# Index-score products of the last block: two single products per tile of the second input projection, instead of three in a row at a tile's end

## The chip, the cores and the metric

The program runs on one core of a Trainium2 chip. The metric is the device time of one execution in microseconds (us), as the median of a few runs. The kernel before takes 2761.79 us (three runs, 2760.8 to 2763.72).

The core's engines work side by side and meet only at semaphores. PE is TensorE, the matrix engine (PEld is its weight loading), ACT is ScalarE, DVE is VectorE, POOL is GpSimd and SP is the engine that starts most DMAs.

## The reference, cut to what matters

The program is three transformer-like blocks over 512 tokens of width 1024. The first two have one form, the third another. The third begins like this:

```python
h = rms_norm_2(x, g_mix_pre[l])
(lru_x, lru_gate, pool_in, q, k, v, q_idx, k_idx, w_idx,
 gate_logits) = split_columns(h @ w_in[l], IN_SIZES)
ua = causal_depthwise_conv(lru_x, conv_w[l], conv_b[l])
ya = rg_lru(ua, lru_w_a[l], ...) * jax.nn.gelu(lru_gate)
yb = multiscale_pool(pool_in, w_pool[l], pool_scale[l])
yc = dsa_attention(q, k, v, q_idx, k_idx, w_idx)
```

and inside `dsa_attention`, for each block of 128 queries:

```python
admissible = key_chunk[None, :] <= q_chunk[:, None]      # chunks of 64 keys
logits = jnp.einsum('bqhd,bsd->bqhs', qib, k_idx_f) * (IDX_DIM ** -0.5)
score = jnp.einsum('bqh,bqhs->bqs', wb * (IDX_HEADS ** -0.5), jax.nn.relu(logits))
score = jnp.where(admissible[None], score, -jnp.inf)
_, sel = lax.top_k(score, top_k)                         # top_k = 128
```

There are 8 index heads of width 64 and 4 blocks of 128 queries. Query block b has 128 (b + 1) keys that matter. Block 0 has no more than 128 of them, so that all that are admissible are selected whatever their score is.

## The kernel before, in words

Activations lie transposed (features on partitions, the 512 tokens along the free axis). Each float32 operand of a projection is split into a high and a low part, and one block of 128 x 128 weights costs three matrix products of 512 columns: high x high, high x low, low x high (lines 568 to 570, function `mac`). A tile of the projection is one bank of PSUM with 128 output features. It sums 8 weight blocks, so it is 24 products in a row.

The second input projection is stage "z2": 23 tiles, numbered 0 to 22. Tiles 4 to 7 give the index queries `qi`, tile 8 the index keys `ki`, tile 9 the values and index weights, tiles 10 to 13 the input of the pooling, 14 to 17 the gate of the recurrence, 18 to 21 the attention queries and 22 the attention keys. Four banks are used in turn, and a tile waits until the one four before it was taken out (`free_bank`, `tile_free`). A unit of weights (16 blocks, two tiles) is loaded by SP, its high part is written by ACT (`split_unit`, line 1099) and its low part by DVE (line 1599). In each engine's program these splits stand behind the evacuation of the tile that frees the buffer, so the order of work is written out by hand and each engine takes it strictly in a row.

The index scores are made beside z2 as items t, eight (one for each head) per query block. An item is one product on PE with only 64 rows of contraction (line 987), on partitions 0 to 63 for even heads and 64 to 127 for odd heads. It is as wide as the keys of its block, 128 to 512 columns, and goes to one of two banks in turn (`SCORES[t % 2]`). ACT takes it out with a Relu into one of two slots of `sq` (line 1496), and DVE multiplies it with its head's weight and adds it to `score` (lines 2107 and 2110). Item t waits on PE until the Relu of item t - 2 is done. The Relu of item t waits until DVE has added item t - 2. In the kernel before there are 32 items, three at the end of each of tiles 11 to 20 and two at the end of tile 21, on all three engines (`idx_items`).

From tile 18 on, DVE also takes one round of the selection of the top 128 per tile (`take_top8`). Later, after the z2 stage, `hide(0)` overwrites the whole score of query block 0 with constants, and the selection rounds work on blocks 1 to 3 only.

Behind z2 comes the stage "lru" with 12 short tiles of one block (three products) each. ACT loads a table of functions (line 1498), splits the last unit of z2's buffers (line 1099), and takes out lru tiles 0 to 3 as `yb_hi`; DVE follows with `yb_lo` (line 2167) and frees the bank. The lru tile 4 waits for the bank of lru tile 0. After it come the merges ("bm2").

Of the kernel before, what the change touches and what calls it, by code (L numbers as in the profile page):

```python
# [11 lines left out]
ACT = mybir.ActivationFunctionType  # L12
AX_X = mybir.AxisListType.X

P = 128
S = 512
# [231 lines left out]
def block_kernel(nc, stream, xT, pT, memT, vec1, gains, cst, pos, out):  # L248
    with ExitStack() as ctx:
# [16 lines left out]
        sq = sb("sq", 108, [2, S])  # L266
# [204 lines left out]
        idx_done = sem("idx_done")  # L471
# [44 lines left out]
        }  # L516


        IDX_FROM, IDX_ITEMS = 11, 32

        def idx_items(n):
            return range(min(3 * max(n - IDX_FROM, 0), IDX_ITEMS), min(3 * max(n - IDX_FROM + 1, 0), IDX_ITEMS))
        assert idx_items(22).stop == IDX_ITEMS


        NORMS = {
# [30 lines left out]
        def _(pe):  # L557
# [17 lines left out]
                    pe.wait_ge(tile_free, c.at("T", st, n - 3))  # L575
                return bank[t % 4]

            def run(c, st, operand, first=0, last=None, width=S, after=None, together=None):


                tiles = TILES[st]
                u0 = c.base[st]["U"]
                ends = {}
                for n, t in enumerate(tiles):
                    for j, b in enumerate(t):
                        ends[b // BLK] = (n, j)
                seen = -1 if first == 0 else tiles[first - 1][-1] // BLK
                if together is not None:
                    seen, first = tiles[together][0] // BLK, together + 2
                    pe.wait_ge(lo_ready, c.at("U", st, seen + 1))  # L590
                    two = [free_bank(c, st, together + n)[:, 0:width] for n in range(2)]
                    for j in range(KD):
                        for n in range(2):
                            xh, xl, need = operand(together + n, j)
                            if need is not None:
                                pe.wait_ge(need[0], need[1])
                            mm = mac(two[n], (u0 + seen) % 2, tiles[together + n][j] % BLK, P, xh, xl, j == 0, j == KD - 1)
                            if j == KD - 1:
                                mm.then_inc(tile_done, 1)
                for n in range(first, len(tiles) if last is None else last):  # L600
                    t = tiles[n]
                    ps = free_bank(c, st, n)[:, 0:width]
                    for j, b in enumerate(t):
                        u = b // BLK
                        if u > seen:
                            pe.wait_ge(lo_ready, c.at("U", st, u + 1))
                            seen = u
                        xh, xl, need = operand(n, j)
                        if need is not None:
                            pe.wait_ge(need[0], need[1])  # L610
                        mm = mac(ps, (u0 + u) % 2, b % BLK, P, xh, xl, j == 0, j == len(t) - 1)
                        if j == len(t) - 1:
                            mm.then_inc(tile_done, 1)
                        elif ends[u] == (n, j):
                            mm.then_inc(part_done, 1)
                    if after is not None:
                        after(n)

# [355 lines left out]
            def after_z2(n):  # L974
                if n == 10:
                    pe.wait_ge(act_took, c.at("A", "z2", 5))
                    for t in range(ST):
                        mm = nc.tensor.transpose(TURNED[:, t * P:(t + 1) * P], vwT[:, t * P:(t + 1) * P], ident)
                    mm.then_inc(vw_turned, 1)
                for t in idx_items(n):  # L980
                    if t == 0:
                        pe.wait_ge(tile_free, c.at("T", "z2", 9))
                    if t >= 2:
                        pe.wait_ge(idx_relu, t - 1)
                    b, hh = t // 8, t % 8
                    r = slice(64 * (hh % 2), 64 * (hh % 2) + 64)
                    nc.tensor.matmul(SCORES[t % 2][:, 0:(b + 1) * P], qi[r, hh // 2, b * P:(b + 1) * P], ki[r, 0:(b + 1) * P],  # L987
                                     start=True, stop=True).then_inc(idx_done, 1)
            run(c, "z2", lambda n, j: (h_hi[:, j, :], h_lo[:, j, :], (res_split, c.at("R", "norm1", j + 1)) if n == 4 else None),
                together=4, after=after_z2)  # L990

            def lru_operand(n, j):
                if n < 4:
# [43 lines left out]
        for table, stages in ((RR1, STAGES1), (RR2, STAGES2)):  # L1037
            n = 0
# [36 lines left out]
        def _(act):  # L1075
# [398 lines left out]
            link(nc.scalar.activation(lruc[:, 2, 0:4], lruc[:, 1, 0:4], ACT.Ln, bias=1.0))  # L1474
            nc.scalar.activation(lruc[:, 3, 0:4], ap4, ACT.Relu, scale=-1.0).then_inc(softplus_ready, 1)

            def evac_z2(n):
                if n < 8:
                    take_hi(c, "z2", n, n - 4, qi[:, n - 4, :])
                elif n == 9:  # L1480
                    take_hi(c, "z2", n, 4, vwT[:, :])
                elif 14 <= n < 18:
                    if n == 14:
                        for j in range(4):
                            split_hi(c, "z2", j, ua_hi[:, j, :], ua[:, j, :], (res_ready, result_value(c, "z2", j)))
                    take_hi(c, "z2", n, n - 9, lg[:, n - 14, :], ACT.Gelu_apprx_tanh)
                elif n == 19:
                    for j in range(4):
                        r = c.base["z2"]["R"] + 4 + j
                        split_hi(c, "z2", 4 + j, pool_hi[:, j, :], res[:, r % 4, :], (res_ready, result_value(c, "z2", 4 + j)))  # L1490
                for t in idx_items(n):
                    act.wait_ge(idx_done, t + 1)
                    if t >= 2:
                        act.wait_ge(idx_added, t - 1)
                    w = (t // 8 + 1) * P
                    nc.scalar.activation(sq[:, t % 2, 0:w], SCORES[t % 2][:, 0:w], ACT.Relu).then_inc(idx_relu, 1)
            stage_loop(c, "z2", evac_z2, 2)
            act.preload_act_table_set("sigmoid_and_others")
            split_unit(c, "z2", SPLIT_LATER["z2"])
# [79 lines left out]
        def _(dve):  # L1579
# [518 lines left out]

            def add_idx(t):

                b, hh = t // 8, t % 8
                w = (b + 1) * P
                dve.wait_ge(idx_relu, t + 1)
                if t == 0:
                    dve.wait_ge(res_ready, result_value(c, "z2", 3))
                if hh == 0:
                    ins = nc.vector.tensor_scalar(score[:, b, 0:w], sq[:, t % 2, 0:w], wsc[:, b, hh:hh + 1], None, ALU.mult)
                else:
                    dve.wait_ge(idx_added, t)
                    ins = nc.vector.scalar_tensor_tensor(out=score[:, b, 0:w], in0=sq[:, t % 2, 0:w], scalar=wsc[:, b, hh:hh + 1],  # L2110
                                                         in1=score[:, b, 0:w], op0=ALU.mult, op1=ALU.add)
                ins.then_inc(idx_added, 1)
# [16 lines left out]
            A_Z2 = {n: n - 4 for n in range(4, 8)} | {9: 4} | {n: n - 9 for n in range(14, 18)}  # L2129

            def evac_z2(n):
                if n in A_Z2:
                    dve.wait_ge(act_took, c.at("A", "z2", A_Z2[n] + 1))
                    pass_on(c, "z2", n)
                    if 4 <= n < 8:
                        conv(n - 4)
                    elif n >= 14:
                        if n == 14:
                            dve.wait_ge(tile_free, c.at("T", "z2", 14))
                        pool(n - 14)  # L2140
                elif 10 <= n < 14:
                    if n == 10:
                        dve.wait_ge(pad_ready, 1)
                    copy_out(c, "z2", n, 0, pz[:, n - 10, PADW:PADW + S], lambda ps: ps[:, :], wait_act=False)
                    if n == 10:
                        dve.wait_ge(vw_turned, 1)
                        link(nc.vector.tensor_copy(vw[:, :, :], TURNED[:, :].rearrange("p (t d) -> p t d", t=ST)))

                        link(nc.vector.tensor_scalar(wsc[:, :, :], vw[:, :, HD:HD + 8], 8 ** -0.5, None, ALU.mult))
                else:  # L2150
                    dst = {8: ki, 22: kk}.get(n)
                    if dst is None:
                        scale_out(c, "z2", n, qd[:, n - 18, :], -ATT["dsa"]["scale"])
                    else:
                        copy_out(c, "z2", n, 0, dst[:, :], lambda ps: ps[:, :], wait_act=False)
                for t in idx_items(n):
                    add_idx(t)
                if n >= 18:
                    if n == 18:
                        dve.wait_ge(idx_added, 16)  # L2160
                        hide(1)
                    take_top8(rounds[n - 18])
            stage_loop(c, "z2", evac_z2, 2)
# [426 lines left out]
```

## Time and profile before

| what | value |
|---|---|
| median of three runs | 2761.79 us |
| the profiled execution, its own time | 2761.74 us |
| its span in the trace | 2759.9 us |
| PE busy | 2682.9 us (97%) |
| DVE busy | 1399.2 us (51%) |
| ACT busy | 1120.1 us (41%) |
| mean granted clock of TensorE | 0.995 |

The span is the time between the first and last instruction in the trace; 1.8 us of the execution's own time lie around it. PE is busy nearly all the time, so that what lengthens or shortens PE's row of work, or makes it stand still, is what counts. Starts of matrix products are measured, while their ends are modelled. So the time that one product costs in a stream is read from the start of one to the start of the next.

### The profile page before, as it was taken

The page shows a single profiled execution, that of the slowest core. Times are in us where ns is not written, and L with a number is a line of the kernel's source. Part 1 is how long each engine was busy: PE and PEld are TensorE (multiplying, and loading weights), DVE is VectorE, ACT ScalarE, POOL GpSimd, SP SyncE. Part 2 cuts the span into 40 slices and gives each one's busy share as a digit, 9 for nine tenths or more (in the row PEclk, how much of TensorE's full clock was granted, in tenths as well). Part 3 has the DMA queues.
Part 4 walks back from the last instruction along what each step waited for, and adds up shares of the span by engine and source line. Part 5 has one row for each costly group of instructions (what it writes and reads, how often), then busy time and mean ns, then how long its engine had stood idle before and what let it go on. Part 6 is the DMA issues. An engine that isn't in the chain of part 4 may idle for free. (4 is left out here: it accounts for less than half of the span.)

```text
span 2759.9 us, 34815 instructions
## 1 busy us (share of the span) xinstructions
PE 2682.9 (97%) x13528; PEld 2173.7 (79%) x13528; DVE 1399.2 (51%) x2075; ACT 1120.1 (41%) x1760; POOL 406.4 (15%) x316
## 2 busy tenths in 40 slices
PE   8999999999999899999999999999999999999997
PEld 6876778888887787677898888777687688888886
DVE  6656544533324665654453432465588536533423
ACT  6446533423224644654343222453635535523221
POOL 5100002211102310000131110231001012311101
PEclk9999999999999999999999999999999999999999
DMA  4320123132332232112322233222232222122232
GB/s 155 124 90 32 47 78 121 61 106 91 103 109 93 85 114 86 46 46 77 107 77 91 93 105 107 92 76 92 77 108 91 73 96 77 55 98 91 94 107 90
DMA packets 37501, 245.76 MB, mean 89 GB/s; under 512 B 4608, under 2 KB 5632, under 8 KB 8448
## 3 DMA queue, kind: packets, MB, share of 16 engines
q1 hardware_dynamic: 33632, 239.09, 25.4%
q10 hardware_dynamic: 3744, 4.94, 0.5%
q8 instruction: 87, 1.43, 0.2%
q14 instruction: 38, 0.31, 0.0%
HBM read 241.91 MB, written 2.10 MB: 88 GB/s over the span
## 5 line engine op out<-in xcount | busy, mean ns | idle before, releaser
L568 PE MATMUL bank<-h_hi,w_hi 128*128 128x512 f32 x1928 | 762.2, 395 | 4.7 <-DVEq L1637 3.4
L570 PE MATMUL bank<-h_hi,w_lo 128*128 128x512 f32 x1928 | 751.7, 390 | 0.0
L569 PE MATMUL bank<-h_lo,w_hi 128*128 128x512 f32 x1928 | 751.3, 390 | 0.0
L1599 DVE TENSOR_TENSOR w_lo<-raw,w_hi 128x2048 fp32r<-128x2048 f32 x130 | 300.9, 2317 | 340.1 <-ACT w_hi L1099 339.7
L568 PEld LDWEIGHTS bank<-h_hi,w_hi 128*128 128x128 f32 x1928 | 362.4, 188 | 90.8 <-issue 17.6
L570 PEld LDWEIGHTS bank<-h_hi,w_lo 128*128 128x128 f32 x1928 | 362.2, 188 | 76.3
L569 PEld LDWEIGHTS bank<-h_lo,w_hi 128*128 128x128 f32 x1928 | 362.7, 188 | 73.4 <-issue 1.4
L1099 ACT ACTIVATE w_hi<-raw 128x2048 fp32r<-128x2048 f32 x151 | 287.8, 1910 | 245.6 <-PE bank L570 237.1
L1611 DVE TENSOR_TENSOR w_lo<-raw,w_hi 128x2048 fp32r<-128x2048 f32 x60 | 137.6, 2293 | 156.1 <-ACT w_hi L1328 156.1
L568 PE MATMUL bank<-a_hi,w_hi 128*128 128x512 f32 x528 | 205.4, 389 | 0.0
L569 PE MATMUL bank<-a_lo,w_hi 128*128 128x512 f32 x528 | 205.4, 389 | 0.0
L570 PE MATMUL bank<-a_hi,w_lo 128*128 128x512 f32 x528 | 205.4, 389 | 0.0
L2264 POOL TENSOR_TENSOR a_lo<-res,a_hi 128x512 f32 x66 | 91.3, 1385 | 614.1 <-ACT a_hi L1324 563.9
L1894 DVE TENSOR_TENSOR res<-bank,rstd 128x512 f32<-128x512 f32 x60 | 41.5, 692 | 235.2 <-PE bank L570 235.2
L1324 ACT ACTIVATE a_hi<-res 128x512 f32 x60 | 37.9, 632 | 293.6 <-DVE res L1897 293.6
L2242 POOL TENSOR_TENSOR m_lo<-res,m_hi 128x512 fp32r<-128x512 f32 x24 | 31.0, 1293 | 815.1 <-ACT m_hi L1147 815.1
L1269 ACT ACTIVATE pT<-bank 128x512 f32<-128x512 f32 (+3 forms) x168 | 83.0, 494 | 136.8 <-PE bank L749 133.8
L570 PEld LDWEIGHTS bank<-a_hi,w_lo 128*128 128x128 f32 x528 | 99.1, 188 | 20.7
L568 PEld LDWEIGHTS bank<-a_hi,w_hi 128*128 128x128 f32 x528 | 99.1, 188 | 20.6
L569 PEld LDWEIGHTS bank<-a_lo,w_hi 128*128 128x128 f32 x528 | 99.1, 188 | 20.3
L1328 ACT ACTIVATE w_hi<-raw 128x2048 fp32r<-128x2048 f32 x60 | 114.1, 1901 | 0.0
L1322 ACT ACTIVATE sg<-sg 128x512 f32<-128x512 f32 x60 | 37.9, 632 | 177.1 <-DVE sg L1891 177.1
(430 smaller groups left out, 4575.7 us busy)
## 6 DMA issues: line engine op xcount, KB each, us to landing
raw<-in_stream SPq DMA_DIRECT2D x226, 1024.0 KB, 4.8
x<-in_xT SPq DMA_DIRECT2D x4, 512.0 KB, 8.7
out_T<-x ACTq DMA_DIRECT2D x8, 256.0 KB, 2.1
p_f<-in_pT ACTq DMA_DIRECT2D x2, 512.0 KB, 4.0
memf<-in_memT ACTq DMA_DIRECT2D x1, 1024.0 KB, 5.1
cst_sb<-in_cst ACTq DMA_DIRECT2D x1, 409.0 KB, 7.4
pos_i<-in_pos ACTq DMA_DIRECT2D x1, 258.0 KB, 6.2
g_in<-in_gains ACTq DMA_DIRECT2D x3, 4.0 KB, 2.4
```

The source lines that it names most:

```text
L568: nc.tensor.matmul(ps, wh, xh, start=start, stop=False)
L569: nc.tensor.matmul(ps, wh, xl, start=False, stop=False)
L570: return nc.tensor.matmul(ps, wl, xh, start=False, stop=stop)
L1099: nc.scalar.activation(home(c, v)[0][:, :], raw[v % 2][:, :], ACT.Copy).then_inc(hi_ready, 1)
L1269: nc.scalar.activation(a["pT"][h % 2][:, 0:n, b * P:(b + 1) * P], TURNED[:, 0:n * P].rearrange("p (t q) -> p t q", t=n), ACT.Copy).then_in ...
L1322: nc.scalar.activation(sg[:, p, :], sg[:, p, :], ACT.Silu).then_inc(act_took, 1)
L1324: nc.scalar.activation(a_hi[:, bass.ds(i * 2 + p, 1), :].rearrange("p a s -> p (a s)"), res[:, p, :], ACT.Copy).then_inc(res_hi, 1)
L1328: nc.scalar.activation(w_hi[v][:, :], raw[v][:, :], ACT.Copy).then_inc(hi_ready, 1)
L1599: nc.vector.tensor_tensor(lo[:, :], raw[v % 2][:, :], hi[:, :].bitcast(F32), ALU.subtract).then_inc(lo_ready, 1)
L1611: nc.vector.tensor_tensor(w_lo[s][:, :], raw[s][:, :], w_hi[s][:, :].bitcast(F32), ALU.subtract).then_inc(lo_ready, 1)
L1894: nc.vector.tensor_tensor(res[:, p, :], bank[(t0 + 2 * p + 1) % 4][:, :], rstd[:, 0, :], ALU.mult).then_inc(tile_free, 1)
L2264: nc.gpsimd.tensor_tensor(a_lo[:, bass.ds(i * 2 + p, 1), :].rearrange("p a s -> p (a s)"), res[:, p, :], a_hi[:, bass.ds(i * 2 + p, 1), :] ...
```

## The change

The items of query block 0 are left out (24 items are left, with 256, 384 and 512 columns, eight of each), and `idx_at` gives block and head of an item. Each of the tiles 11 to 22 has two items: one behind weight block j = 3, which is the middle of the tile, and one behind j = 7, its end. PE gets the first through a new hook `within` in `run`. ACT and DVE have the first item ahead of their evacuation of the same tile, and the second behind it.

```diff
-        IDX_FROM, IDX_ITEMS = 11, 32
-        def idx_items(n):
-            return range(min(3 * max(n - IDX_FROM, 0), IDX_ITEMS), min(3 * max(n - IDX_FROM + 1, 0), IDX_ITEMS))
+        IDX_FROM, IDX_ITEMS, IDX_AFTER = 11, 24, (3, 7)
+        def idx_item(n, half):
+            t = 2 * (n - IDX_FROM) + half
+            return [t] if 0 <= t < IDX_ITEMS else []
+        def idx_at(t):
+            return t // 8 + 1, t % 8
...
                             mm.then_inc(part_done, 1)
+                        if within is not None:
+                            within(n, j)
...
-                for t in idx_items(n):
+            def within_z2(n, j):
+                for t in idx_item(n, IDX_AFTER.index(j)) if j in IDX_AFTER else ():
                     if t == 0:
                         pe.wait_ge(tile_free, c.at("T", "z2", 9))
                     if t >= 2:
                         pe.wait_ge(idx_relu, t - 1)
-                    b, hh = t // 8, t % 8
+                    b, hh = idx_at(t)
...
+            def relu_idx(t):
+                act.wait_ge(idx_done, t + 1)
+                if t >= 2:
+                    act.wait_ge(idx_added, t - 1)
+                w = (idx_at(t)[0] + 1) * P
+                nc.scalar.activation(sq[:, t % 2, 0:w], SCORES[t % 2][:, 0:w], ACT.Relu).then_inc(idx_relu, 1)
+
             def evac_z2(n):
+                for t in idx_item(n, 0):
+                    relu_idx(t)
...
-                for t in idx_items(n):
+                for t in idx_item(n, 1):
+                    relu_idx(t)
             stage_loop(c, "z2", evac_z2, 2)
             act.preload_act_table_set("sigmoid_and_others")
...
             def evac_z2(n):
+                for t in idx_item(n, 0):
+                    add_idx(t)
...
-                for t in idx_items(n):
+                for t in idx_item(n, 1):
                     add_idx(t)
                 if n >= 18:
                     if n == 18:
-                        dve.wait_ge(idx_added, 16)
+                        dve.wait_ge(idx_added, 8)
```

The order on PE around the end of tile 11, before (h_hi, h_lo are the activations, w_hi, w_lo the weights of z2, `ki` and `qi` the index keys and queries):

```order
L570 MATMUL bank3<-h_hi_56,w_lo1_54 128x512
L987 MATMUL bank4<-ki_138,qi_136 128x128 [waits tile_free]
L987 MATMUL bank5<-ki_138,qi_136 128x128
L987 MATMUL bank4<-ki_138,qi_136 128x128 [waits idx_relu]
L568 MATMUL bank0<-h_hi_56,w_hi0_51 128x512 [waits lo_ready,tile_free]
```

The three items stand in a row between the last product of one tile and the first of the next. The order on PE now, at the end of one of the later tiles and in the middle of the next:

```order
L996 MATMUL bank5<-ki_138,qi_136 128x512 [waits idx_relu]
L573 MATMUL bank1<-h_hi_56,w_hi0_51 128x512 [waits tile_free]
...
L575 MATMUL bank1<-h_hi_56,w_lo0_53 128x512
L996 MATMUL bank4<-ki_138,qi_136 128x512 [waits idx_relu]
L573 MATMUL bank1<-h_hi_56,w_hi0_51 128x512
L574 MATMUL bank1<-h_lo_57,w_hi0_51 128x512
```

Each item now has full-height products on both sides, and no item has another one next to it.

The order on PE now, at the border of z2's last tile and lru's first (`pool_hi`, `pool_lo` are the operands of lru):

```order
L575 MATMUL bank2<-h_hi_56,w_lo1_54 128x512
L996 MATMUL bank5<-ki_138,qi_136 128x512 [waits idx_relu]
L573 MATMUL bank3<-pool_hi_144,w_hi0_51 128x512 [waits res_split,lo_ready,tile_free]
L574 MATMUL bank3<-pool_lo_145,w_hi0_51 128x512
L575 MATMUL bank3<-pool_hi_144,w_lo0_53 128x512
```

The last item has come to stand behind z2's last tile, where lru's first product followed at once before.

The order on ACT at this border before, from the last items (of tile 21) to the first output of lru:

```order
L1496 ACTIVATE sq_61<-bank4 128x512 [waits idx_added,idx_done]
L1496 ACTIVATE sq_61<-bank5 128x512 [waits idx_added,idx_done]
L1099 ACTIVATE w_hi0_51<-raw0_49 128x2048 [waits raw_ready0,tile_done]
L1498 ACT_TABLE_LOAD
L1099 ACTIVATE w_hi1_52<-raw1_50 128x2048 [waits raw_ready1,tile_done]
L1108 ACTIVATE yb_hi_152<-bank3,cst_sb_70 128x512 [waits tile_done]
```

The order on ACT at the same border now:

```order
L1492 ACTIVATE sq_61<-bank5 128x512 [waits idx_added,idx_done]
L1108 ACTIVATE w_hi0_51<-raw0_49 128x2048 [waits raw_ready0,tile_done]
L1492 ACTIVATE sq_61<-bank4 128x512 [waits idx_added,idx_done]
L1492 ACTIVATE sq_61<-bank5 128x512 [waits idx_added,idx_done]
L1513 ACT_TABLE_LOAD
L1108 ACTIVATE w_hi1_52<-raw1_50 128x2048 [waits raw_ready1,tile_done]
L1117 ACTIVATE yb_hi_152<-bank3,cst_sb_70 128x512 [waits tile_done]
```

Two Relus, those of tile 22's items, have moved between the split of tile 21 and the table load.

## Rows read from the trace of the kernel before

**Rows 1.** Stretches (from:to, length, PE busy, its instructions, granted clock, DMA share, GB/s):
```profile
1886.00:1970.00 84.00, 79.23 (x332) 1.00 0.21 73
```

**Rows 2.** Waits of PE in that stretch (us in total, times, longest):
```profile
PE bank L987 <- ACT sq L1496: 4.8, 10, 0.7
```

**Rows 3.** Timeline of PE, end of tile 11 (start, us, what, idle before):
```profile
1889.99 0.39 PE L570 MATMUL bank<-h_hi,w_lo 128*128 128x512 f32 x1
1890.31 0.49 PE L987 MATMUL bank<-ki,qi 64*128 64x128 f32 x4
1891.16 0.48 PE L987 MATMUL bank<-ki,qi 64*128 64x128 f32 x2 [0.36 <-ACT sq L1496]
1891.58 0.50 PE L568 MATMUL bank<-h_hi,w_hi 128*128 128x512 f32 x1
```

**Rows 4.** Timeline of PE, an item with 256 and one with 384 columns:
```profile
1912.53 0.70 PE L987 MATMUL bank<-ki,qi 64*128 64x256 f32 x2 [0.47 <-ACT sq L1496]
1913.15 0.50 PE L568 MATMUL bank<-h_hi,w_hi 128*128 128x512 f32 x1
...
1935.44 0.91 PE L987 MATMUL bank<-ki,qi 64*128 64x384 f32 x2 [0.57 <-ACT sq L1496]
1936.28 0.50 PE L568 MATMUL bank<-h_hi,w_hi 128*128 128x512 f32 x1
```

**Rows 5.** Timeline of PE, end of tile 19; the first row is of 1949.94 to 1950.00 alone:
```profile
1949.94 0.70 PE L987 MATMUL bank<-ki,qi 64*128 64x512 f32 x2
...
1951.74 1.12 PE L987 MATMUL bank<-ki,qi 64*128 64x512 f32 x2 [0.68 <-ACT sq L1496]
1952.80 0.50 PE L568 MATMUL bank<-h_hi,w_hi 128*128 128x512 f32 x1
```

**Rows 6.** Timeline of PE, end of tile 21 to the first tiles of bm2:
```profile
1966.67 0.39 PE L570 MATMUL bank<-h_hi,w_lo 128*128 128x512 f32 x1
1966.99 1.13 PE L987 MATMUL bank<-ki,qi 64*128 64x512 f32 x4
1968.05 0.50 PE L568 MATMUL bank<-h_hi,w_hi 128*128 128x512 f32 x1
...
1973.41 0.39 PE L570 MATMUL bank<-h_hi,w_lo 128*128 128x512 f32 x1
1973.68 0.47 PE L568 MATMUL bank<-pool_hi,w_hi 128*128 128x512 f32 x1
...
1976.29 0.39 PE L570 MATMUL bank<-pool_hi,w_lo 128*128 128x512 f32 x1
1977.59 0.50 PE L568 MATMUL bank<-ua_hi,w_hi 128*128 128x512 f32 x1 [0.91 <-DVE yb_lo L2167]
...
1983.18 0.39 PE L568 MATMUL bank<-h_hi,w_hi 128*128 128x512 f32 x1
...
1988.62 0.39 PE L568 MATMUL bank<-yb_hi,w_hi 128*128 128x512 f32 x1
```

**Rows 7.** Timeline of ACT, 1968 to 1977 us:
```profile
1968.15 1.09 ACT L1496 ACTIVATE sq<-bank 128x512 f32<-128x512 f32 x2 [6.12 <-PE bank L987]
...
1971.06 1.28 ACT L1498 ACT_TABLE_LOAD   x1
1973.84 1.92 ACT L1099 ACTIVATE w_hi<-raw 128x2048 fp32r<-128x2048 f32 x1 [1.50 <-PE bank L570]
1975.66 1.83 ACT L1108 ACTIVATE yb_hi<-bank,cst_sb 128x512 fp32r<-128x512 f32 x3
```

**Rows 8.** Timeline of DVE, 1973.5 to 1982 us:
```profile
1976.78 2.73 DVE L2167 SCALAR_TENSOR_TENSOR yb_lo<-bank,cst_sb,yb_hi 128x512 fp32r<-128x512 f32 x4 [1.40 <-ACT yb_hi L1108]
```

**Rows 9.** Stretches of 2 us, PE alone (columns as in Rows 1):
```profile
2182.00:2184.00 2.00, 0.66 (x11) 0.94 0.00 0
2184.00:2186.00 2.00, 1.31 (x8) 0.50 0.00 0
...
2190.00:2192.00 2.00, 2.00 (x9) 0.86 0.00 0
```

**Rows 10.** Timeline of PE, a single longer wait in the second block:
```profile
1767.67 0.47 PE L568 MATMUL bank<-h_hi,w_hi 128*128 128x512 f32 x1 [1.71 <-DVEq L1637]
```

More of the change, by code:

```diff
@@ L516, in block_kernel @@
         }
-        IDX_FROM, IDX_ITEMS = 11, 32
-        def idx_items(n):
-            return range(min(3 * max(n - IDX_FROM, 0), IDX_ITEMS), min(3 * max(n - IDX_FROM + 1, 0), IDX_ITEMS))
-        assert idx_items(22).stop == IDX_ITEMS
+        IDX_FROM, IDX_ITEMS, IDX_AFTER = 11, 24, (3, 7)
+        def idx_item(n, half):
+            t = 2 * (n - IDX_FROM) + half
+            return [t] if 0 <= t < IDX_ITEMS else []
+        assert idx_item(22, 1) == [IDX_ITEMS - 1]
+        def idx_at(t):
+            return t // 8 + 1, t % 8
         NORMS = {
@@ L576, in free_bank, with run @@
                 return bank[t % 4]
-            def run(c, st, operand, first=0, last=None, width=S, after=None, together=None):
+            def run(c, st, operand, first=0, last=None, width=S, after=None, together=None, within=None):
                 tiles = TILES[st]
@@ L989, in _ @@
             run(c, "z2", lambda n, j: (h_hi[:, j, :], h_lo[:, j, :], (res_split, c.at("R", "norm1", j + 1)) if n == 4 else None),
-                together=4, after=after_z2)
+                together=4, after=after_z2, within=within_z2)
             def lru_operand(n, j):
@@ L1490, in evac_z2 @@
                         split_hi(c, "z2", 4 + j, pool_hi[:, j, :], res[:, r % 4, :], (res_ready, result_value(c, "z2", 4 + j)))
-                for t in idx_items(n):
[L1492 to L1496, printed above, removed]
+                for t in idx_item(n, 1):
+                    relu_idx(t)
             stage_loop(c, "z2", evac_z2, 2)
@@ L2099, in add_idx @@
             def add_idx(t):
-                b, hh = t // 8, t % 8
+                b, hh = idx_at(t)
                 w = (b + 1) * P
```

## The prediction

> **What bounds the kernel now.** I first read the stretch in which the index items stand. PE is busy 79.23 of 84 us there, at full clock (2.4 GHz) [rows 1], so PE's own row of work sets the time. I then read what PE waits for in it: ten short waits for the Relu of an index item, 4.8 us in all, and nothing else [rows 2]. The third view is PE's timeline around the items, read from start to start. It has the two facts on which everything rests.
>
> The first is what a plain tile costs. In bm2 a tile of 24 full-height products goes from 1983.18 to 1988.62, 5.44 us, or 0.227 us a product [rows 6].
>
> The second is that two items side by side cost what one costs. An item is two passes on 64 rows. At 1949.94 two passes start within 0.06 us of each other [rows 5]: they belong to an even and an odd head, that is to the lower and the upper half of the array, and they run together. The group of two items behind tile 21 (x4) holds PE from 1966.99 to 1968.05, 1.06 us [rows 6]. The single item at 1951.74 (x2) holds it from there to 1952.80, which is 1.06 us too [rows 5]. So each old group of three is a pair for the price of one, a wait, and then a single one.
>
> The last view is the border between z2 and lru. PE stops there until 1977.59 for DVE's `yb_lo` [rows 6], which waited for ACT's `yb_hi` [rows 8], which waited for ACT's split, which starts 0.2 us after z2's last tile has ended [rows 7]. So ACT bounds this border, and what is put ahead of that split is late one for one.
>
> **The change part by part.** First the old cost of the items on PE. From the last product of tile 11 (1889.99) [rows 3] to that of tile 22 (1973.41) [rows 6] are 83.42 us. Eleven plain tiles are 11 x 5.44 = 59.84. The 32 items with their waits cost 23.58 us.
>
> Then the new cost. What one item holds PE, from its start to the next full-height product, is 0.62 us with 256 columns and 0.84 with 384 [rows 4], and 1.06 with 512 [rows 5]. Going into and out of such an item costs a little more. Tile 22 with its pair is 1973.41 - 1966.67 = 6.74 us, less 5.44 and 1.06 leaves 0.24 us per group [rows 6]. Before there were 11 groups, now there are 24, since each item is a group of its own. A lone item is then 0.86, 1.08 or 1.30 us. Up to the end of tile 22 there are 23 of them: 8 x 0.86 + 8 x 1.08 + 7 x 1.30 = 24.62 us. The old waits go entirely, because an item's predecessor but one is now a whole tile (over 7 us) back and not 0.85 us [rows 3]. The narrow items of query block 0 go as well. Yet the sum is +1.04 us up to the end of tile 22: 21 slots of PE time (eleven pairs, ten single items) become 24, the cheapest ones (128 columns, 0.42 us from 1891.16 to 1891.58) [rows 3] are those that vanish, and 13 more entries are paid.
>
> The trace shows no item in the middle of a tile, so that its entry cost is bounded: from below by nothing (12 x 0.24 = 2.9 us less), from above by 0.74 us more each, which is what a third item at tile 19 stood behind the end of its pair (1951.74 - 1949.94 - 1.06) [rows 5], if the Relu were not in time. I take 0.24, since what surrounds it is the same kind of product as at a tile's end; and the Relu would have to be late by most of a tile, while ACT's longest single piece there is the split of 1.92 us [rows 7].
>
> Here a rule can be weighed. The trace shows 0.24 us per change between the 64-row and the 128-row form at tile ends [rows 6]. The Trainium skill (TensorEngine Tiling (Array Packing), Key Properties) says that changing the tiling mode drains TensorE, wherever this is. By that rule 24 entries are paid and the sum stays; with an entry free inside a tile it would be the 2.9 us less of rival two. The same skill (TensorE: Matmul & The Clock Gate, Part 3, Packing small matmuls) says that small products in different row groups run together and that a single one is no faster than a full-height one, and this speaks against taking the pairs apart; the trace agrees, 1.06 us for both.
>
> The border to lru comes next. Call the end of tile 22's last product E; before, E = 1973.41 + 0.23 = 1973.64. PE went on with lru's fifth tile at 1977.59, E + 3.95 [rows 6]. Now the last item stands there. It starts at E + 0.09 (as 1966.99 - 1966.67 - 0.23). Its Relu starts 1.16 us later (1966.99 to 1968.15) [rows 6, 7], at E + 1.25, and ends at about E + 1.85 (two take 1.09 us) [rows 7]. Only then comes the table load, 1.28 us, which before lay at 1971.06 under tile 22 and cost nothing [rows 7]. The split starts at E + 3.15 and lets `yb_hi` start 1.82 us later (1973.84 to 1975.66), at E + 4.97. From there to PE it is 1977.59 - 1975.66 = 1.93 us as before: E + 6.90. That is 2.95 us more. The last item itself (1.15 us of PE) is in it. PE's stall grows from 1977.59 - 1976.29 - 0.23 = 1.07 us to about 2.9. DVE has one addition, the copy of `kk` and a selection round there, which end well before `yb_lo` could start.
>
> I cost the rest at nothing. DVE's and ACT's items of tiles 11 to 21 are hidden by PE's tiles of over 7 us. POOL's splits of `ua` and `pool` start up to some 3 us later and are wanted tiles later. DMA moves nothing else, and SP's queue waits for the same splits. The rest of the block follows PE and ACT together, so I see nothing that gives the shift back.
>
> The sum is +1.04 + 2.95 = +4.0 us. The profiled execution took 2761.74 us of its own (span 2759.9), 0.05 below the median of the runs shown, so the forecast is 2765.7 us.
>
> **The rivals.** One: the clock falls at the longer stall, and the kernel is measurably slower. After a thin stretch with PE busy 0.66 of 2 us the granted clock fell to 0.50 (1.2 GHz) and was back only after 2190 [rows 9]. Three stretches at 0.50 and parts of two are some 6.4 us at half speed, 3.2 us of work. If lru's stall of 2.9 us does the same, the time is 2761.74 + 4.0 + 3.2 = 2768.9. For it: this stall is longer than any in [rows 2, 10]. Against it: single waits of 1.71 us [rows 10] and the present 1.07 us did not do it in these stretches. It decides as soon as PE's clock in lru is below 1.
>
> Two: the middle of a tile costs no entry. Then it is 2.9 us less, 2762.8. For it: there is no wait for a new weight unit or bank in the middle. Against it: the 0.24 us come with the change of form.
>
> Three: the border is not late by all of it, since ACT's table load or split finds another place than in my chain. With only the last item's 1.15 us left of the 2.95 the time would be 2763.9. Against it: ACT works strictly in its written order, and the new last Relu stands ahead of both.
>
> Four, on the faster side: a lone item costs half a pair, as one would expect who takes the pair's time for two products in a row. The slots to E, 24.62 - 23 x 0.24 = 19.10, would be halved and the last item too: 4.0 - 9.55 - 0.5 = -6.1 us, 2755.6. Against it stands the single item of 1.06 us [rows 5].
>
> **How the numbers follow.** My forecast has 0.57, rival one 0.16, two 0.12, three 0.09 and four 0.06. About 0.2% of the time (5.5 us) is what a measurement can tell from no change. The forecast, 2765.7, is 3.9 us over the median and inside that, its own spread of about 1.3 us reaches beyond it a little (0.03). So slower is 0.16 + 0.03 = 0.19, faster 0.06, and the same 0.75. The range from 2762.7 to 2769.0 takes in rivals one to three and leaves out four and the far tails.
>
> **What would show it.** Right, if the items stand on PE with full-height products behind them after 0.62, 0.84 and 1.06 us; if the wait for the Relu is gone; if tile 19 with its two items has 5.44 + 2 x 1.30 = 8.0 us; and if lru's fifth tile starts some 6.9 us after z2's last product, with the table load behind the last Relu. Wrong, if the lone items hold PE for half of this, if ACT or DVE make PE wait inside z2, or if the granted clock falls behind the border.

## The result and the profile after

The changed kernel takes 2768.38 us (median of 16 runs, 2767.26 to 2772.01), the kernel before 2763.11 us (16 runs). The ratio is 1.0020, with a 95% interval from 1.0013 to 1.0027: about 5.3 us more, where 3.9 were forecast over the median of three runs that was then shown (2761.79). The time lies in the stated range, and 5.3 us is just under the 5.5 us that the prediction took for no change; the interval leaves out 1, so a small loss is measured.

The two programs differ in one short piece. In every trace there are three marks for it: the four transposes on PE behind z2's tile 10, the end of tile 22's last product (E, its start + 0.23), and lru's fifth tile, the first product with `ua_hi`. A fourth is the product in bm2 for which PE waits on a weight split. Here are the first and the last mark of the kernel before, from PE's timeline (start, us, what, idle before):

```profile
1884.31 0.60 PE L978 MATMUL bank<-cst_sb,vwT 128*128 128x128 f32 x4
...
2006.07 0.47 PE L568 MATMUL bank<-yb_hi,w_hi 128*128 128x512 f32 x1 [0.96 <-DVE w_lo L1599]
```

The same timeline of the kernel after, with all marks:

```profile
1886.37 0.60 PE L985 MATMUL bank<-cst_sb,vwT 128*128 128x128 f32 x4
...
1976.54 0.39 PE L575 MATMUL bank<-h_hi,w_lo 128*128 128x512 f32 x1
1976.86 1.12 PE L996 MATMUL bank<-ki,qi 64*128 64x512 f32 x2
1977.91 0.50 PE L573 MATMUL bank<-pool_hi,w_hi 128*128 128x512 f32 x1
...
1980.55 0.39 PE L575 MATMUL bank<-pool_hi,w_lo 128*128 128x512 f32 x1
1983.32 0.50 PE L573 MATMUL bank<-ua_hi,w_hi 128*128 128x512 f32 x1 [2.38 <-DVE yb_lo L2184]
...
2013.40 0.47 PE L573 MATMUL bank<-yb_hi,w_hi 128*128 128x512 f32 x1 [0.96 <-DVE w_lo L1614]
```

From first to last mark the piece takes 127.03 us against 121.76 before: 5.27 us more, as much as the two medians differ. That the two agree so well is partly luck: the two profiled executions are 8.1 us apart (spans 2759.9 and 2768.0), 2.06 of it ahead of the first mark and 0.77 behind the last, where the instructions are the same. The first mark lies anywhere from 1884.31 to 1887.00 in the ten profiles told here, so what stands outside the piece is left out below. The 5.27 us fall into three parts. z2 takes 1976.77 - 1886.37 = 90.40 us against 1973.64 - 1884.31 = 89.33 (+1.07). The border to lru takes 6.55 us against 3.95 [rows 6] (+2.60). From lru's fifth tile to the last mark it is 30.08 us against 28.48 (+1.60).

Inside z2 no item makes PE wait any more; the 4.8 us of [rows 2] are gone. This is the whole list of PE's waits from 1886 to 1985:

```profile
PE bank L573 <- DVE yb_lo L2184: 2.4, 1, 2.4
```

The items stand alone, as the first one in the middle of tile 11 and one of 384 columns show; compare [rows 3, 4]:

```profile
1889.67 0.70 PE L996 MATMUL bank<-ki,qi 64*128 64x256 f32 x2
1890.30 0.50 PE L573 MATMUL bank<-h_hi,w_hi 128*128 128x512 f32 x1
...
1922.17 0.91 PE L996 MATMUL bank<-ki,qi 64*128 64x384 f32 x2
1923.01 0.50 PE L573 MATMUL bank<-h_hi,w_hi 128*128 128x512 f32 x1
```

They hold PE for 0.63 and 0.84 us, and the one at 1976.86 for 1.05: the prices of [rows 4, 5]. Tile 19 with its two items takes 8.02 us (1945.81 to 1953.83), where 8.0 was forecast. At the border ACT's timeline answers to [rows 7]:

```profile
1978.02 0.60 ACT L1492 ACTIVATE sq<-bank 128x512 f32<-128x512 f32 x1 [3.41 <-PE bank L996]
1978.64 1.28 ACT L1513 ACT_TABLE_LOAD   x1
1979.93 1.91 ACT L1108 ACTIVATE w_hi<-raw 128x2048 fp32r<-128x2048 f32 x1
1981.75 2.40 ACT L1117 ACTIVATE yb_hi<-bank,cst_sb 128x512 fp32r<-128x512 f32 x4
```

Counted from E = 1976.77 these are +1.25, +1.87, +3.16 and +4.98. The third part is the clock, in stretches of 2 us (from:to, length, PE busy, its instructions, granted clock, DMA share, GB/s):

```profile
1982.00:1984.00 2.00, 0.68 (x3) 1.00 0.00 0
1984.00:1986.00 2.00, 2.00 (x7) 0.53 0.00 0
1986.00:1988.00 2.00, 2.00 (x7) 0.62 0.03 8
1988.00:1990.00 2.00, 2.00 (x10) 1.00 0.71 156
```

PE stands still for 1983.32 - 1980.55 - 0.23 = 2.54 us, its stall. Behind it the granted clock goes to half (1.2 GHz). It stays there for 3.4 us: a mean of 0.53 over 2 us is 1.88 us at half clock, and one of 0.62 is 1.52.

### The profile page after: what moved, and what is told of

The parts are those of the page before. It is cut to its first block and busy times, and to the rows that moved or that the text cites. A ratio compares the mean times of both kernels' runs of the same rounds, so it can differ in the third digit from the quotient of the medians.

```text
span 2768.0 us, 34750 instructions
## 1 busy us (share of the span) xinstructions
PE 2693.5 (97%) x13512; PEld 2176.9 (79%) x13512; DVE 1394.4 (50%) x2067; ACT 1118.8 (40%) x1752; POOL 405.1 (15%) x316
```

## The experiments

Two theories stood at the start. A: the loss is 1.07 us of lone items, 2.60 of border and 1.60 of clock behind the longer stall. B: the clock dip is chance, as it is in other places of both traces, and a third of the loss lies somewhere else. The table has all runs. The columns from z2 to sum are read off each run's one profile at the marks above; PE's stall is a part of the border. The ratio (with its 95% interval) is that of the timed runs.

| kernel | z2 | border | PE's stall there | to the last mark | sum | against before (121.76) | ratio of times |
|---|---|---|---|---|---|---|---|
| before | 89.33 | 3.95 | 1.07 | 28.48 | 121.76 | | 1 |
| changed | 90.40 | 6.55 | 2.54 | 30.08 | 127.03 | +5.27 | 1.0020 (1.0013 to 1.0027) |
| e0, changed again | 90.38 | 6.55 | 2.54 | 30.07 | 127.00 | +5.24 | 1.0017 (1.0008 to 1.0026) |
| e1, last Relu late | 90.37 | 5.08 | 1.06 | 28.49 | 123.94 | +2.18 | 1.0007 (0.9998 to 1.0016) |
| e7, border free | 90.40 | 3.60 | 0.88 | 28.51 | 122.51 | +0.75 | 0.9998 (0.9989 to 1.0007) |
| e5, before, table load late | 89.35 | 5.37 | 2.49 | 29.96 | 124.68 | +2.92 | 1.0008 (0.9999 to 1.0017) |
| e3, before, fewer items | 86.12 | 3.59 | 0.87 | 28.52 | 118.23 | -3.53 | 0.9981 (0.9972 to 0.9990) |
| e2, pairs in the middle | 78.80 | 3.60 | 0.87 | 28.51 | 110.91 | -10.85 | 0.9954 (0.9941 to 0.9968) |
| e6, pairs at the end | 77.52 | 7.04 | 3.02 | 29.84 | 114.40 | -7.36 | 0.9962 (0.9949 to 0.9976) |
| e4, pairs of one half | 86.26 | 3.59 | 0.87 | 28.49 | 118.34 | -3.42 | 0.9974 (0.9965 to 0.9984) |

**e0: the changed kernel again.**

> The changed kernel once more, for a second profile and a time on the same chip as the next three. Theory A (1.07 us more in z2, 2.60 us more at the border to lru, and 1.6 us because the longer stall there halves the clock for some products): 5.3 us over before, and the profile has a granted clock below 1 in the 4 us behind the border again. Theory B (the clock dip in the first profile was a chance event like those elsewhere, and the last third of the difference lies somewhere else): no dip behind the border, lru's fifth tile some 28.5 us ahead of the third merge tile's second half, and still 5.3 us over before.

Measured: 2767.98 us against 2762.65. The dip is there again, at the same place:

```profile
1982.00:1984.00 2.00, 1.77 (x6) 0.81 0.00 0
1984.00:1986.00 2.00, 2.00 (x6) 0.50 0.03 8
1986.00:1988.00 2.00, 2.00 (x9) 0.84 0.34 57
```

The three parts repeat within 0.02 us. B falls. What the clock did here in the executions that were not profiled isn't known; three of e0's eleven took only 2763.2 to 2764.5 us.

**e1: the last Relu behind the table load and the split.**

```diff
-                for t in idx_item(n, 1):
+                for t in idx_item(n, 1) if n < 22 else ():
                     relu_idx(t)
             stage_loop(c, "z2", evac_z2, 2)
             act.preload_act_table_set("sigmoid_and_others")
             split_unit(c, "z2", SPLIT_LATER["z2"])
+            relu_idx(IDX_ITEMS - 1)
```

> The changed kernel, but on ACT the Relu of the last item stands behind the table load and the split, and not ahead of them. Theory A: yb_hi starts at the end of z2 + 2.6 us (2.0 as before, and one Relu), lru's fifth tile at + 4.2, PE stalls there for under 0.3 us, the clock does not fall, and 3.9 us of the 5.3 come back: 1.4 us over before. Rival (the loss is the lone items inside z2, and the border would be hidden anyway): no change against the changed kernel, 5.3 us over before.

Measured: 2764.92 us. 3.1 us of the 5.2 come back and not 3.9. The clock stays full, but the stall is 1.06 us and not under 0.3. The stretches around it:

```profile
1978.00:1980.00 2.00, 1.46 (x7) 1.00 0.00 0
1980.00:1982.00 2.00, 1.63 (x7) 1.00 0.00 0
1982.00:1984.00 2.00, 2.00 (x11) 1.00 0.04 8
```

DVE's timeline shows what my chain had left out:

```profile
1977.92 0.75 DVE L2126 SCALAR_TENSOR_TENSOR score<-sq,wsc,score 128x512 f32<-128x512 f32 x1 [1.74 <-ACT sq L1492]
1978.59 0.42 DVE L2140 MAX8 top<-score 128x8 f32<-128x256 f32 x1
1979.05 0.09 DVE L2141 MATCH_VALUE_LOAD score<-top,score 128x8 f32 x1
1979.12 0.41 DVE L2141 MATCH_REPLACE8 score<-top,score 128x256 f32<-128x256 f32 x1
1979.57 2.73 DVE L2185 SCALAR_TENSOR_TENSOR yb_lo<-bank,cst_sb,yb_hi 128x512 fp32r<-128x512 f32 x4
```

The last item's addition and a selection round stand ahead of `yb_lo`, wait for the Relu that is now late, and end only just before 1979.57. `yb_hi` starts at 1977.78, and in the changed kernel `yb_lo` follows its start by 0.77 us. The wait went from ACT to DVE.

**e7: both items of tile 22 in its middle**, the rest as in the changed kernel.

```diff
             t = 2 * (n - IDX_FROM) + half
+            if n == 22:
+                return [t, t + 1] if half == 0 else []
             return [t] if 0 <= t < IDX_ITEMS else []
```

> The changed kernel, but both items of tile 22 stand in its middle. Theory A: z2 is 1.0 to 1.1 us longer than in before, the border is as in before (lru's fifth tile at the end of z2 + 3.6 to 4.0), no clock dip: 0.7 to 1.1 us over before, some 4.2 us under the changed kernel. Rival (the loss is not at the border): 5 us over before.

Measured: 2762.3 us against 2763.45, no difference that can be told from none. In its profile z2 is 90.40 us, the border 3.60 and there is no dip: with one item moved by half a tile 4.5 us of the 5.3 are gone, and the +0.75 left is what was expected. So 1.07 us is the price of the lone items against the old groups, and the rest is the border with its clock dip. The border is 0.35 us shorter here than before, and 2.95 shorter than in the changed kernel.

**e5: the kernel before, the table load behind the split.**

```diff
-            act.preload_act_table_set("sigmoid_and_others")
             split_unit(c, "z2", SPLIT_LATER["z2"])
+            act.preload_act_table_set("sigmoid_and_others")
```

> The kernel before with one edit on ACT: the table load at the border to lru stands behind the split and not ahead of it. Theory A: yb_hi is late by the load's 1.28 us, PE's stall grows from 1.07 to some 2.3 us, and a stall of this length halves the clock for some products, 1.6 us as in the changed kernel: 2.9 us over before. Rival (the clock falls in the changed kernel for the 64-row items ahead of the stall, not for the stall): full clock behind the border, 1.3 us over before.

Measured: the stall is 2.49 us, and the clock halves with it, though no item stands anywhere near. PE's timeline:

```profile
1979.00 0.39 PE L570 MATMUL bank<-pool_hi,w_lo 128*128 128x512 f32 x1
1981.72 0.80 PE L568 MATMUL bank<-ua_hi,w_hi 128*128 128x512 f32 x1 [2.33 <-DVE yb_lo L2167]
1982.32 0.63 PE L569 MATMUL bank<-ua_lo,w_hi 128*128 128x512 f32 x1
1982.74 0.63 PE L570 MATMUL bank<-ua_hi,w_lo 128*128 128x512 f32 x1
```

The clock is at half before PE goes on:

```profile
1980.00:1982.00 2.00, 0.28 (x1) 0.86 0.23 94
1982.00:1984.00 2.00, 2.00 (x5) 0.50 0.00 0
```

A mean of 0.86 is 0.56 us at half clock, of which 0.28 lie ahead of PE's start at 1981.72 if the clock stays down, as the next row has it. The last two products above stand 0.42 us apart in place of 0.23. The piece is 2.92 us longer, as A has it. So the dip needs the stall and not the items before it. The timed runs say less, +0.9 us in the medians (2764.37 against 2763.45), with an interval from -0.3 to +4.7 us that holds both nothing and the 2.9. The profiles show one way for this to come about: before has a clock dip in a later, unrelated stretch, which e5 and e4 don't have. The rows are of before, e4 and e5 in this order:

```profile
2170.00:2210.00 40.00, 37.21 (x195) 0.91 0.24 80
```

```profile
2170.00:2210.00 40.00, 37.30 (x207) 1.00 0.23 80
```

```profile
2170.00:2210.00 40.00, 37.22 (x221) 1.00 0.19 62
```

A mean of 0.91 over 40 us is some 7 us at half clock, and from the last mark to the end of the span before takes 2759.9 - 2006.07 = 753.8 us, e5 750.9 and e4 750.8. That is 3 us of time. The timed executions of these kernels may have had that dip or not, and what decides it was not tried.

**e3: the kernel before without the items of query block 0**, which leaves out no part of the output (the shift of the block stands in the widths and in DVE's addition too).

```diff
-        IDX_FROM, IDX_ITEMS = 11, 32
+        IDX_FROM, IDX_ITEMS = 11, 24
...
-                    b, hh = t // 8, t % 8
+                    b, hh = t // 8 + 1, t % 8
```

> The kernel before with only the eight items of query block 0 left out: 24 items, three in a row at the end of tiles 11 to 18. Theory A: eight groups of pair, wait and single cost about 20.4 us in place of 23.58, the border is as before: 3.1 us under before, so that the changed kernel's placement alone costs some 8.4 us. Rival (the dropped items were covered by waits that only change their place): within 1 us of before.

Measured: 2757.8 us, 4.9 us under before; z2 is 3.21 us shorter, 3.1 was expected. By the medians it is 1.3 us more than by the marks, and the 95% interval (2.8 to 7.7 us under before) holds both. So the new placement alone, against the same items three in a row, costs 127.03 - 118.23 = 8.8 us in the piece, although 4.3 us of waits for the Relu are still in e3.

**e2: pairs in the middle of the tiles.**

```diff
         def idx_item(n, half):
-            t = 2 * (n - IDX_FROM) + half
-            return [t] if 0 <= t < IDX_ITEMS else []
+            t = 2 * (n - IDX_FROM)
+            return [t, t + 1] if half == 0 and 0 <= t < IDX_ITEMS else []
```

> The 24 items in pairs (an even and an odd head side by side) in the middle of tiles 11 to 22, nothing at a tile's end. Theory A (what counts is the number of slots and entries): 12 groups cost 4 x 0.86 + 4 x 1.08 + 4 x 1.30 = 12.96 us in place of 23.58, PE waits for no Relu, the border is as in before: 10.6 us under before. Rival (an item costs the same alone or beside another, and only the waits and the border matter): about 1 us over before.

Measured: 2748.88 us, 13.8 us under before and the fastest kernel of all here. z2 is 10.53 us shorter, 10.6 was expected, and the whole piece 10.85. The other 2.9 us of the medians are not in the piece, and where they are isn't shown; the interval, 8.8 to 16.3 us, holds the 10.85. PE's timeline in tile 22:

```profile
1960.19 1.13 PE L996 MATMUL bank<-ki,qi 64*128 64x512 f32 x4
1961.25 0.50 PE L573 MATMUL bank<-h_hi,w_hi 128*128 128x512 f32 x1
```

Two items hold PE for 1.06 us, what one does. PE's only wait from 1886 to 1970 is the border's:

```profile
PE bank L573 <- DVE yb_lo L2184: 0.7, 1, 0.7
```

**e4: the same pairs, both items on the same 64 rows.** The sums over heads are taken in another order.

```diff
-            return t // 8 + 1, t % 8
+            return t // 8 + 1, (0, 2, 4, 6, 1, 3, 5, 7)[t % 8]
```

> The pairs in the middle of tiles 11 to 22, but with the heads taken in the order 0, 2, 4, 6, 1, 3, 5, 7, so that the two items of a pair need the same 64 rows of the array. Theory A (a pair is cheap because its two items run at once on the two halves): each pair takes two slots, 4 x (0.62 + 0.84 + 1.06) = 10.1 us more than with an even and an odd head (2748.9 there), so within 2 us of before. Rival (it is cheap because two items stand side by side and share entry and exit): as fast as the other pairs, 12 to 14 us under before.

Measured: z2 is 7.46 us longer than with an even and an odd head, the rest is the same. PE's timeline in the same tile:

```profile
1960.72 1.98 PE L996 MATMUL bank<-ki,qi 64*128 64x512 f32 x4
1962.63 0.50 PE L573 MATMUL bank<-h_hi,w_hi 128*128 128x512 f32 x1
```

Two items on one half hold PE for 1.91 us. Side by side is not enough: the two halves of the array make the pair cheap. My 10.1 us were too many, since a second item in a row on the same half costs 0.85 and not 1.06; why is not shown. The time, 2757.19 us, is 6.3 us under before where within 2 was expected. By the marks it is 3.4, and the profile of e4 has 3.0 us less than that of before behind the last mark, where the dip just told is missing. That the timed executions differ by that dip too is likely from this, not shown.

**e6: pairs at the end of the tiles.**

```diff
         def idx_item(n, half):
-            t = 2 * (n - IDX_FROM) + half
-            return [t] if 0 <= t < IDX_ITEMS else []
+            t = 2 * (n - IDX_FROM)
+            return [t, t + 1] if half == 1 and 0 <= t < IDX_ITEMS else []
```

> The 24 items in pairs of an even and an odd head at the end of tiles 11 to 22. Theory A: 12.96 us of items as in the middle (a group costs the same at either place), but the last pair stands behind tile 22, and its two Relus, the table load and the split are in a row before yb_hi: about 0.5 us more than the changed kernel's border, lru's fifth tile at the end of z2 + 7, a clock dip behind it, so 5 to 6 us over the pairs in the middle and 7 to 8 under before. Rival (entering from inside a tile is dearer or cheaper than from its end): tiles 12 to 21 differ in length from those of the pairs in the middle.

Measured: 2754.1 us, 9.4 under before, 7.4 by the marks. z2 up to E has eleven pairs and 77.52 us; with the last one, 1.30, it is 78.82, against 78.80 with the pairs in the middle. A group costs the same at either place. The border is E + 7.04 as forecast, its stall 3.02 us, and the clock dips (29.84 us to the last mark). The piece is 3.5 us longer than with the pairs in the middle, and not 5 to 6: the last pair is part of the border now, and z2 is 1.3 us shorter for it. (The medians differ by 5.2.)

## Why the prediction was right, point by point

**What bounds.** PE's row of work in z2 and ACT's at the border, as said. e7 moves one item and takes the whole loss at the border away. e1 moves only a Relu and takes 3.1 us away where 3.9 were expected, since DVE's addition behind that Relu came to bound the border in ACT's place.

**The lone items.** 24.62 - 23.58 = +1.04 us were forecast, +1.07 measured, and all four profiles with lone items have 90.37 to 90.40 us. The slot of 1.06 us for one or two, on which it rests, is shown by e2 (two halves) against e4 (one half). The entry cost in the middle is the 0.24 taken, so rival two falls: e6 and e2 differ by 0.02 us over eleven groups. The rule of the Trainium skill (TensorEngine Tiling (Array Packing), Key Properties) that a change of the tiling mode drains TensorE agrees with this: the change is paid at both places, 0.24 us each time. Two smaller slips: up to E there are 23 slots and 12 entries more than before, not 24 and 13 (the sum itself uses 23); and the 1.06 us "for both" compares a lone item with a pair, so that a lone one is no faster than a full-height product of its kind is in no row here.

**The waits.** Gone entirely, as said, and they were worth less than the pairs that were taken apart for it: the same items in threes, waits included, take 4.3 us less in z2 (e3, 86.12 against 90.40).

**The border.** The chain on ACT was forecast at E + 1.25, + 1.85, + 3.15 and + 4.97, and measured at + 1.25, + 1.87, + 3.16 and + 4.98. Only its last step was too long: from `yb_hi` to PE I took 1.93 us from before, and it is 1.57 now. So the term was +2.60 and not +2.95. The step is 1.93 to 1.94 us in before and e5 and 1.57 to 1.58 in the changed kernel, e2, e3, e4, e6 and e7. The former two have all 32 items. e3, which has before's order with 24, has the short step, so it goes with the number of items and not with their place; why stays open. Against e7, which has the short step too, the last item costs 6.55 - 3.60 = 2.95 us at the border, just what was forecast for it.

**What the sum lacked.** The forecast's own sum, +4.0, comes to +3.67 in the profile. The remaining 1.60 us is rival one, to which I gave 0.16: the clock falls at the longer stall. It fell in each of the four profiles with a stall of 2.49 to 3.02 us at the border and in none of the six with 0.87 to 1.07. This term stood at nothing in the sum, and it should have stood there. The measured 2768.38 is nearer to rival one's 2768.9 than to the forecast's 2765.7. Of the 2.7 us between forecast and time, 1.3 is the median of before, which is 2763.11 over 16 runs and 2761.79 over the first three. The rest is mostly the clock's 1.60, less the 0.35 at the border.

The price of rival one was too high. [rows 9] give 0.24 + 6 + 0.56 = 6.8 us at half clock, and not the 6.4 read from them, so 3.4 us of work; the dip here lasts 3.4 us and costs 1.60. Part of the luck is here: a dip of the full price would have made the kernel slower by more than the 5.5 us that were called no change.

The argument against rival one, that single waits of 1.71 us did not do it, was weak for a stall half as long again. The traces show more: a wait of this length does it at times. At the same place of the third block, behind full work, PE waits 1.75 us in the changed kernel and 1.76 before. PE's timeline of the changed kernel, and of before:

```profile
2140.99 0.71 PE L734 MATMUL bank<-kk,qd 64*128 64x128 f32 x4 [1.75 <-DVE st_neg L1852]
```

```profile
2133.72 0.49 PE L727 MATMUL bank<-kk,qd 64*128 64x128 f32 x4 [1.76 <-DVE st_neg L1837]
```

In the 4 us behind this wait the granted clock is 0.57 in the changed kernel, e0 and e1, 0.66 in e7, and 1.00 in the other six profiles. What decides it there stays open, and so it is not shown that a stall of 2.5 us at the border must always bring the dip.

**Rivals three and four.** ACT's timeline has the table load and the split where the chain has them, and with the Relu moved out of the way (e1) the time moves, so rival three falls. Rival four, a lone item at half a pair's price, is refuted by every row of one.

## What to carry to other kernels

Before small products are spread out to avoid a wait, look whether two of them run at once on two halves of the array (two starts at one time, x4 in the time of x2): taking such a pair apart costs a whole product, which can be more than the wait. The gain was to be had by keeping the pair and moving it to where its results are not late, one pair per tile in the middle (10.9 us in the piece, 13.8 by the medians). And what is put behind the last tile of a stage can push all that stands behind it on the next engine: here one small product cost 2.95 us in this way, and the clock 1.6 us more once the stall had grown to 2.5 us.

## What the runs showed of the hardware

A stall of PE of 2.5 to 3.0 us between full work went with half clock in four profiles of four (products 0.42 us apart, not 0.23), which cost 1.3 to 1.6 us beside the stall. One of 0.9 to 1.1 us at the same place did not in six of six, and one of 1.75 us at another place did in four of ten. The clock fell behind PE's restart in the changed kernel and e0, and ahead of it in e5 and e6 (granted clock 0.86 and 0.79 in the stretch with the restart). A 64-row float32 product of 512 columns holds PE 1.06 us, two on different halves 1.06 us, and two on the same half 1.91 us. Going from 128-row to 64-row products and back cost 0.24 us, in the middle of a tile as at its end.
